# V rows weighted by ScalarE and added by the Pool for three of ten expert blocks, their token rows held in PSUM

## What is computed

```
x = x + g1 * mixer(norm(x) * (1 + sc1) + sh1)
h = norm(x) * (1 + sc2) + sh2
idx, gate = 16 best of 128 x 128 experts, for each of 8 heads      # 128 slots per token
act  = gelu(einsum('thkd,td->thk', u_tab[idx], h))
x = x + g2 * einsum('thk,thkd->td', gate * act, v_tab[idx])
```

## Time and profile before

| | |
|---|---|
| median of 3 runs (lowest to highest) | 4979.95 us (4967.22 to 4985.87) |
| the profiled execution | 4967.69 us, span 4965.9 us |
| PE busy | 3861.3 us (78%), of which L680 in 5120 records |
| DVE busy | 3242.6 us (65%) |
| POOL busy | 1447.9 us (29%), all but the first 0.5 us of it gathers |
| ACT busy | 748.0 us (15%) |
| DMA | 1497.72 MB, mean 302 GB/s |
| granted TensorE clock, mean | 0.929 |

### The profile page before, as it was taken

The page is one execution under the profiler, slowest core; times in us unless marked ns, Lnnn a source line. Parts: engine busy times, 40 slices in busy tenths (PEclk is TensorE's granted clock), DMA queues, the critical chain, the costliest instruction groups (busy, mean ns, idle before and its releaser), DMA issues. The chain is left out here.

```text
span 4965.9 us, 36487 instructions
## 1 busy us (share of the span) xinstructions
PE 3861.3 (78%) x11046; PEld 1898.0 (38%) x11046; DVE 3242.6 (65%) x8263; ACT 748.0 (15%) x2211; POOL 1447.9 (29%) x1284
## 2 busy tenths in 40 slices
PE   7588678988777776788868786788977687777776
PEld 6464334643222222235535443346422222222222
DVE  1546765536887868854574766664378787687666
ACT  0111124211101010010121112341010100100101
POOL 0001112212454434432222021221044354354432
PEclk9788788999999999999989897899999999999999
DMA  8334456754998999999969254566389899899998
GB/s 266 99 116 178 153 188 242 252 194 192 412 415 368 421 374 414 421 390 387 365 245 366 97 203 146 206 253 220 127 354 421 365 419 421 362 421 421 407 421 341
DMA packets 342149, 1497.72 MB, mean 302 GB/s; under 512 B 31424, under 2 KB 176448, under 8 KB 178112
## 3 DMA queue, kind: packets, MB, share of 16 engines
q0 software_dynamic: 184320, 1342.26, 67.4%
q1 hardware_dynamic: 157632, 153.13, 9.6%
HBM read 1491.97 MB, written 3.31 MB: 301 GB/s over the span
## 5 line engine op out<-in xcount | busy, mean ns | idle before, releaser
L680 PE MATMUL expert_acc<-uv_ring,diag 128*128 128x512 f32 x3744 | 1865.1, 631 | 417.9 <-DVE diag L1227 407.8
L634 POOL DMA_INDIRECT uv_ring<-uv,expert_index x936 | 1050.2, 1122 | 2717.1 <-PE expert_acc L680 2174.4
L680 PEld LDWEIGHTS expert_acc<-uv_ring,diag 128*128 128x128 f32 x3744 | 688.1, 198 | 1487.8 <-DVE diag L1227 898.5
L1218 DVE CUSTOM_DVE_ANT_0 uv_ring<-uv_ring,arena 128x1024 f32<-128x1024 f32 x680 | 831.5, 1223 | 243.2 <-DMA uv_ring<-uv,expert_index 240.5
L680 PE MATMUL expert_acc<-arena,diag 128*128 128x512 f32 x1376 | 687.8, 632 | 264.2 <-DVE diag L1227 196.3
L951 ACT ACTIVATE gelu<-u_dot 128x1 f32<-128x1 f32 x1280 | 256.0, 203 | 2943.8 <-DVE u_dot L1218 2943.2
L1227 DVE TENSOR_SCALAR diag<-const_mats,expert_gate,gelu 128x128 f32<-128x128 f32 x1280 | 465.7, 364 | 308.8 <-ACT gelu L951 214.1
L634 POOL DMA_INDIRECT arena<-uv,expert_index x344 | 397.6, 1156 | 757.2 <-PE expert_acc L680 460.3
L1218 DVE CUSTOM_DVE_ANT_0 arena<-arena 128x1024 f32<-128x1024 f32 x344 | 420.8, 1223 | 172.6 <-DMA arena<-uv,expert_index 171.2
L680 PEld LDWEIGHTS expert_acc<-arena,diag 128*128 128x128 f32 x1376 | 243.4, 195 | 698.1 <-DVE diag L1227 425.2
L1218 DVE CUSTOM_DVE_ANT_0 uv_ring<-uv_ring,prompt_rows 128x1024 f32<-128x1024 f32 x256 | 312.1, 1219 | 113.4 <-DMA uv_ring<-uv,expert_index 112.9
(11 more groups left out here) (202 smaller groups left out, 2785.0 us busy)
## 6 DMA issues: line engine op xcount, KB each, us to landing
w_ring<-w_ada SPq DMA_DIRECT2D x66, 512.0 KB, 11.3
w_ring<-w_in SPq DMA_DIRECT2D x64, 512.0 KB, 5.0
w_ring<-w_pq SPq DMA_DIRECT2D x64, 512.0 KB, 4.5
w_ring<-w_out SPq DMA_DIRECT2D x32, 512.0 KB, 6.3
uv_ring<-w_ada SPq DMA_DIRECT2D x30, 512.0 KB, 5.3
uv_ring<-uv,expert_index POOLq DMA_INDIRECT x936, 11.7
arena<-b_ada SPq DMA_DIRECT2D x48, 128.0 KB, 6.2
arena<-uv,expert_index POOLq DMA_INDIRECT x344, 15.7
```

Source lines behind the costliest of these rows:

```text
L634: pool.indirect_dma_start(out=UV[j], out_offset=None, in_=uv, in_offset=bass.IndirectOffsetOnAxis(ap=idxs[:, n % 2, k:k + 1], axis=0)).the ...
L680: ins = pe.matmul(acc[:, half, :], diag[:, m % DIAGS, :], UV[SLOT_AT[m]][:, D + 512 * half:D + 512 * half + 512], start=(k == 0), stop=(k ...
L1218: V_.tensor_tensor_reduce(UV[j][:, 0:D], UV[j][:, 0:D], rows_of(n), 1.0, 0.0, ALU.mult, ALU.add, dots[:, m % DOTS:m % DOTS + 1]).then_inc( ...
```

## The change

For blocks 0, 4 and 5 (`summed_by_pool`) the V half of a slot goes another way. ACT makes a column from gelu and gate and scales the slot's V rows by it in place, 128x1024 (`weigh` of ACT). POOL adds the scaled rows to `pacc`, a sum in SBUF that a memset has cleared (`add_row`), and increments `s_vs` in PE's stead. In POOL's queue the add of a slot stands ahead of the gather that goes into the buffer it has just read. DVE makes no diagonals and PE multiplies no V rows for these blocks; the diagonals of the others are numbered anew (`diag_turn`). `add_peer` takes the sum from `pacc` in two operations of 1024 columns.

The token rows of these blocks are transposed by PE straight into the two accumulator banks, which are free while POOL sums (`rows_to_psum`), and DVE's dots read them there. The `ht` tiles and their drains by ACT go for these blocks; the waits on them become waits on `s_prow`. `htok_p` gives its place to `pacc`. The diff, cut to what matters:

```diff
-    "wo": (4, 16), "n2": (2, 8), "pq": (16, 16), "ps": (4, 16), "ht": (2, 8),
+    "wo": (4, 16), "n2": (2, 8), "pq": (16, 16), "ps": (4, 16), "ht": (0, 8),
...
+LESS = {"ht": (2, 0)}
...
+def summed_by_pool(n):
+    return n % NBLK == 0 or n == NBLK - 1
+def diag_turn(n, k):
+    return sum(SLOTS for x in range(n) if not summed_by_pool(x)) + k
...
+        weight = sb("expert_weight", [P, DOTS])
...
-        htok_p = sb("prompt_rows", [P, D])
+        pacc = sb("pool_sum", [P, D])
...
+            def add_row(n, k):
+                m = n * SLOTS + k
+                if k == 0:
+                    if n:
+                        pool.wait_ge(s_pup.sem, n)
+                    nc.gpsimd.memset(pacc[:], 0.0).then_inc(pool_chain, 1)
+                    pool.wait_ge(pool_chain, sum(summed_by_pool(x) for x in range(n + 1)))
+                else:
+                    pool.wait_ge(s_vs, m)
+                pool.wait_ge(s_pw, sum(SLOTS for x in range(n) if summed_by_pool(x)) + k + 1)
+                nc.gpsimd.tensor_tensor(pacc[:], UV[SLOT_AT[m]][:, D:2 * D], pacc[:], ALU.add).then_inc(s_vs, 1)
...
+                        added = 0
                         for k in range(SLOTS):
                             m = n * SLOTS + k
                             j = SLOT_AT[m]
+                            while summed_by_pool(n) and n * SLOTS + added <= SLOT_BEFORE[m]:
+                                add_row(n, added)
+                                added += 1
...
+                        while summed_by_pool(n) and added < SLOTS:
+                            add_row(n, added)
+                            added += 1
...
-                pe.wait_ge(s_dg, m + 1)
+                pe.wait_ge(s_dg, diag_turn(n, k) + 1)
                 for half in range(2):
-                    ins = pe.matmul(acc[:, half, :], diag[:, m % DIAGS, :], UV[SLOT_AT[m]][:, D + 512 * half:D + 512 * half + 512],
+                    ins = pe.matmul(acc[:, half, :], diag[:, diag_turn(n, k) % DIAGS, :], UV[SLOT_AT[m]][:, D + 512 * half:D + 512 * half + 512],
...
-                if 2 <= m <= SLOTS + 1:
+                if 2 <= m <= SLOTS + 1 and not summed_by_pool(n):
                     add_v(n, m - 2)
+            def rows_to_psum(n, b):
+                if n:
+                    if summed_by_pool(n - 1):
+                        pe.wait_ge(s_dot, n * SLOTS)
+                    else:
+                        pe.wait_ge(s_pup.sem, n)
+                for c in range(DC):
+                    ins = turn(acc[:, c // 4, (c % 4) * P:(c % 4 + 1) * P], hT[:, c, b * P:(b + 1) * P])
+                ins.then_inc(s_prow, 1)
...
-                        for half in range(0 if first else 2):
+                        for half in range(0 if first or summed_by_pool(blk(l, g, b)) else 2):
...
+                        rows_to_psum(blk(l, 0, 0), 0)
...
+                            rows_to_psum(n, b)
...
+            def weigh(n, k):
+                m = n * SLOTS + k
+                act.wait_ge(s_gel, m + 1)
+                chain(nc.scalar.activation(weight[:, m % DOTS:m % DOTS + 1], gel[:, m % DOTS:m % DOTS + 1], ACT.Copy,
+                                           scale=gat[:, n % 2, k:k + 1]))
+                v = UV[SLOT_AT[m]][:, D:2 * D]
+                nc.scalar.activation(v, v, ACT.Copy, scale=weight[:, m % DOTS:m % DOTS + 1]).then_inc(s_pw, 1)
             def gelu_beside(n, m):
                 if m < SLOTS:
                     gelu(n, m)
+                    if summed_by_pool(n):
+                        weigh(n, m)
...
-                return htok[(n % NBLK - 1) % 2] if n % NBLK else htok_p[:]
+                return acc[:].rearrange("p a n -> p (a n)") if summed_by_pool(n) else htok[(n % NBLK - 1) % 2]
...
-                tmp = psum_out if g else htok_p[:, 0:512]
                 dve.wait_ge(s_vs, (n + 1) * SLOTS)
+                if summed_by_pool(n):
+                    chain(V_.tensor_tensor(pacc[:], pacc[:], G[:, gate_tile(n // NBLK, 1, g), :], ALU.mult))
+                    V_.tensor_tensor(X[:, n % NBLK, :], X[:, n % NBLK, :], pacc[:], ALU.add).then_inc(s_pup.sem, 1)
+                    return
+                tmp = psum_out
...
-                if 1 <= m <= SLOTS:
+                if 1 <= m <= SLOTS and not summed_by_pool(n):
...
-                    dve.wait_ge(*full["ht"].at(l - 1, 1, 7))
+                    dve.wait_ge(s_prow, 2 * l)
...
-                        dve.wait_ge(*free["ht"].at(l, 0, 1))
+                        dve.wait_ge(s_prow, 2 * l + 1)
...
-                        dve.wait_ge(*free["ht"].at(l, g, 2 * b + 1))
                         if b + 1 == nb and l + 1 < L:
                             add_peer(n - 1)
+                            dve.wait_ge(s_prow, 2 * l + 2)
                             beside.start(n, BESIDE_PROMPT)
                             continue
+                        dve.wait_ge(*free["ht"].at(l, g, 2 * b + 1))
```

More of the change, by code:

```diff
@@ L267, in psum_order @@
             out += [("n2", l, g, i) for i in range(2 * nb)]
-            out += [("pq", l, g, i) for i in range(8)] + [(s, l, g, i) for s in ("ht", "ps") for i in range(2)]
+            out += [("pq", l, g, i) for i in range(8)] + [(s, l, g, i) for s in (("ht", "ps") if g else ("ps",)) for i in range(2)]
             out += [("pq", l, g, i) for i in range(8, 16)] + [("ps", l, g, 2), ("ps", l, g, 3)]
             for b in range(1, nb):
-                out += [("ht", l, g, 2 * b), ("ht", l, g, 2 * b + 1)]
+                if not summed_by_pool(l * NBLK + FIRST_BLOCK[g] + b):
+                    out += [("ht", l, g, 2 * b), ("ht", l, g, 2 * b + 1)]
                 out += [("ps", l, g, 4 * b + i) for i in range(4)]
@@ L286, in build, with __init__ @@
         class Stage:
-            def __init__(self, name, n=(1, 1), step=1):
+            def __init__(self, name, n=(1, 1), step=1, less=()):
                 self.sem = ctx.enter_context(nc.semaphore(name))
-                self.n, self.step = n, step
+                self.n, self.step, self.less = n, step, less
             def at(self, l, g=0, i=0):
-                return self.sem, (l * sum(self.n) + (self.n[0] if g else 0) + i + 1) * self.step
+                before = sum(self.less[:l]) if self.less else 0
+                return self.sem, (l * sum(self.n) + (self.n[0] if g else 0) + i + 1 - before) * self.step
         acc = ctx.enter_context(nc.psum_tensor("expert_acc", [P, 2, 512], F32))
         rot = ctx.enter_context(nc.psum_tensor("rotating", [P, BANKS, 512], F32))
-        full = {s: Stage(f"{s}_full", n) for s, n in FULL_COUNTS.items()}
-        free = {s: Stage(f"{s}_drained", n) for s, n in FULL_COUNTS.items()}
+        full = {s: Stage(f"{s}_full", n, less=LESS.get(s, ())) for s, n in FULL_COUNTS.items()}
+        free = {s: Stage(f"{s}_drained", n, less=LESS.get(s, ())) for s, n in FULL_COUNTS.items()}
         def tile(s, l, g, i):
@@ L1122, in drain_scores @@
                                 act.wait_ge(s_dot, (blk(l, g, b) - 1) * SLOTS)
-                            nc.scalar.activation((htok[b % 2] if g else htok_p[:])[:, 512 * half:512 * half + 512], t, ACT.Copy).then_inc(free["ht"].sem, 1)
+                            nc.scalar.activation(htok[b % 2][:, 512 * half:512 * half + 512], t, ACT.Copy).then_inc(free["ht"].sem, 1)
                         for k in range(first, last):
```

4 lines of the change are left out of this document (3 added, 1 removed).

## The result

The changed kernel takes **5041.83 us** (median of 4 runs, 5033.65 to 5047.48) against 4982.91 for the kernel before, run beside it: a ratio of **1.0123**, 95% interval 1.0106 to 1.0139. The loss is small, but clear of the noise. The profiled execution spans 5042.1 us, 76 more than before's 4965.9.

What follows compares the result with a forecast made beforehand. PE was taken to bound the projections, DVE the taps, a three-engine chain scan and heads, mostly DMA the middle stage. Two stages at -56 us, then -5, +3, +2, gave -112 us: forecast 4870 us, range 4770 to 5030.

Steps and rivals of the forecast that it cites:

- Pool's add and cycle: Pool's queue: an add of 2.44 us, with gather issue and handover a cycle of 3.9 us per slot.
- Output and query projection: First and third stage: PE sets the pace and Pool's cycle is next, so -20 us for each projection.
- Pool becomes the engine that bounds: Rival, Pool's queue: adds delay gathers, slower above a 4.55 us cycle, 5125 us at the high end; chance 0.15.
- Input projection: First and third stage: PE-bound, 12 slots at 1.71 us each, -20 us a stage.
- Pool and DVE beside each other: Taps and scan: Pool's adds cost DVE 0.6 us for each of 33 slots, +20 us a stage.
- Taps, scan, norm and keys: First and third stage: DVE loses diagonals, ACT takes PE's place in scan, PE partly relieved; -3, -5, -5 us.
- Heads: Attention heads, 36 slots: PE loses 62 us, ACT gains 52, Pool needs 140; near the old time, 0.
- the clock: PE with emptier heads: matmuls at 1.2 GHz on the chain, +2 us.
- Middle stage: Block 4: nothing to win in modulation, -5 us in the prompt mixer, +3 for one new wait.
- The relief: Work taken off for 384 slots: 1.71 us of PE and 0.26 us of DVE a slot.
- adds and DVE shut each other out: Rival, taps and scan: each of 33 slots costs DVE 2.44 us, +80 a stage, total 4990 us; chance 0.14.
- Relief in full: Rival, whole kernel: add near 1.22 us, no cost beside DVE, -240 us to 4740; chance 0.13.

Runs made afterwards that it cites:

- e1: The changed kernel with the Pool's add cut to 8 of 1024 columns, most of the V sum left out: 4856.36 us, ratio 0.9748.
- e6: The changed kernel with both the Pool's add and ScalarE's weighting cut to 8 of 1024 columns: 4785.91 us, ratio 0.9615.
- e7: The changed kernel with block 4 left as before, only the prompt's blocks 0 and 5 changed: 4996.52 us, ratio 1.004.
- e2: The changed kernel with each Pool add replaced by two memsets of the accumulator, which only write: 4856.05 us, ratio 0.9747.

## Why the prediction was wrong

By its own steps, for a beside stage (forecast, measured from the table):

- **Pool's add and cycle**: 2.44 us, 2.378 measured; a cycle of 3.9, 3.6 measured. Right. In both projections the Pool works almost without a pause, 2.36 of add, 0.27 of handover and 0.95 of gather:

```profile
1008.94 2.36 POOL L650 TENSOR_TENSOR pool_sum<-uv_ring,pool_sum 128x1024 f32<-128x1024 f32 x1
1011.58 0.95 POOL L671 DMA_INDIRECT uv_ring<-uv,expert_index  x1 [0.27 <-POOL pool_sum L650]
1012.55 2.37 POOL L650 TENSOR_TENSOR pool_sum<-uv_ring,pool_sum 128x1024 f32<-128x1024 f32 x1
```

- **Output and query projection**: -20 and -20, measured -23 and -25. Right. PE is full (58.0 of 58) and so, nearly, is the Pool; with the add narrow they take 57.8 and 55.9 us instead of 58.0 and 58.5, so the Pool costs some 3 us here. The rival *Pool becomes the engine that bounds* did not occur: its zero was at an add of 3.1 us. That the time has its sign is chance.
- **Input projection**: -20, measured -21, but in part by luck. With the add narrow it is -29.5: ten DVE records lose 20 us in it, of which 8 reach its length, and the forecast had neither.
- **Pool and DVE beside each other**: +20 a stage, none in the middle one. *This is the step that failed.* Against the run with the narrow add the first stage loses 79 us and the third 75. I let only the 33 slots of taps and scan pay, 0.6 us each. Both factors were too small. The 32 adds that ran in these parts stretched DVE's records by 58 us, 1.8 a slot, of which 35 reach their length (22 in the taps, 5 up to the scan, 8 in it). The other 44 us stand where I had put nothing, since stretched records stand in every part but the query projection: 23 us in the heads, 8 in the input projection, 7 in norm and keys, and 6 from the output to the query projection, some of it the Pool's queue. I had split the slots into those where DVE sets the pace and those where it does not; but in a chain over three engines none sets the pace, and a stretched link can lengthen it.
- **Taps, scan, norm and keys**: -3, -5, -5 without that cost; e1 and e6, free of it, have the taps at +2 and +1, the scan at -4 and -13, norm and keys at +7 and +1. With it +24, +4, +14. (In the scan's working, 3058.9 and three times 1.65 give 3063.9, not 3064.1; the -5 would be -7.)
- **Heads**: 0, measured +38. Two errors: the adds (187.9 to 164.9 in e1: 23 us), and ScalarE's weighting (164.9 to 153.5 in e6: 11 us), which I had argued away by a step with two slots that would be 7.0 us long where it had been 7.1. I read from this that the chain goes through ScalarE's queue and had no slack there; no run moved the weighting to see. The last 3.5 us stay open; the clock, for which I had allowed +2 in all, is one candidate.
- **Middle stage**: -5, measured +50. Modulation kept its 197 us, as forecast. The mixer did not: to the scan +26, scan and norm +14, heads +9, the rest +1. My argument went by the Pool's cycle and the bytes in flight and left the DVE term out, though the adds stretched records by 67 us there too. With the add narrow the mixer is back (343 us against 347 before and 397 after); e7 confirms the place.
- **What of 315 us reaches the end**: 186, so about six tenths, if all of the 186 is put down to the stretched records. That is net of 19 us by which modulation is longer in e1. The rest of the 315 lies beside other waits.
- **The relief**: without the term for Pool and DVE my sum was -152. Relief alone measures -193 (e6), and the weighting, which I had put at next to nothing outside the scan, +67: two errors that partly hide each other. 4982 - 152 = 4830, where e1 measured 4856.

The rival *adds and DVE shut each other out* named the mechanism, with the sign to look for (records longer than now), and gave 4990. Its 80 us a stage are close to the 79 and 75 measured, but by luck: it had them all in taps and scan, where 35 stand, and none in the middle stage. *Relief in full* gave 4740 for a change without these costs; e6 took 4786.

What stays open: why modulation takes 216 us in e1 and 221 in e6, where the Pool's adds are short, against 197 before and after. Its DMA share falls there from 1.01 to 0.94 and 0.89. In e2, where memsets fill the Pool's queue, it takes 199, which points to how early the gathers are issued; no run tests it. Nor was it tried to give ScalarE's weighting another place in its queue.

## What to carry to other kernels

Before moving work to the Pool, count *all* DVE instructions with two SBUF operands that run beside it, small ones too, and price each Pool instruction that meets one at a good part of its own length on DVE (here 1.8 of 2.4 us), wherever a chain passes through DVE, not only where DVE is full. Look for the loss in the duration of DVE's records, since no wait or idle time shows it. Where an engine is full in one part only, move the work in that part alone and to an engine that is idle there: 64 slots on DVE, with the accumulator in PSUM, gave 2.1%, and 384 on ScalarE and Pool cost 1.2%.

## What the runs showed of the hardware

- A Pool add of 128x1024 fp32 from SBUF takes 2378 ns, of 8 columns 272, of 256 columns 725 (794 in the mean, which has its waits for DVE in it); a memset of 128x1024 takes 955. Half of the 4497 ns that the Trainium skill (GPSIMD Engine Reference, Performance versus the Vector engine) gives for 2048 elements was the prediction's estimate of 2.25 us, and the trace has 6% more.
- A Pool instruction that reads SBUF and a DVE instruction with two SBUF operands are not served together: a DVE product of 128x16 took 2.97 us beside an add and 0.17 alone, and an add that met running taps 2.78 instead of 2.35. All 174 stretched records outlast the add. Beside memsets nothing is stretched but a few copies and TENSOR_SCALARs.
- Not only two-input instructions are held. In the kernel after, a TENSOR_SCALAR of four columns took 2.72 us and ended with the Pool's add:

```profile
778.96 2.72 DVE L1545 TENSOR_SCALAR stats<-stats 128x4 f32<-128x4 f32 x1 [9.43 <-ACT hT L1124]
779.30 2.35 POOL L650 TENSOR_TENSOR pool_sum<-uv_ring,pool_sum 128x1024 f32<-128x1024 f32 x1
```

- DVE multiplies by a column and adds to PSUM in one instruction of 1289 ns for 128x1024, against 1224 for a product of two SBUF operands.
